# Head 0's path to the first expert gathers is reordered: output products, search over the corner of the sums, sample mixing, softmax halves

## The reference, cut to what matters

```python
h = rmsnorm(x)
gate_a, gate_b, z, xBC, dt, c_q, c_kv, k_rope = split(h @ w_in)
A = ssd_branch(z, xBC, dt)          # gated, group-normed, @ w_ssm_proj
B = mla_attention(c_q, c_kv, k_rope, cached pages)   # @ w_mla_proj
x = x + (sigmoid(gate_a) * A + sigmoid(gate_b) * B) @ w_out
x = x + peer(rmsnorm(x))
# peer, for each of 8 heads:
q = tb @ wq;  s1, s2 = q[:128] @ keys0, q[128:] @ keys1
sc1, i1 = top_k(s1, 16);  sc2, i2 = top_k(s2, 16)
sc, sel = top_k(sc1[:, None] + sc2[None, :], 16)     # 16 of 256 sums
idx = i1 * 128 + i2 at sel                            # 16 of 16384 experts
out += sum_k softmax(sc)_k * gelu(u[idx_k] . tb) * v[idx_k]
```

## Time and profile before

| | us |
|---|---|
| median of 3 runs | 2122.85 |
| lowest and highest | 2122.74, 2126.36 |
| span of the profiled execution, first to last instruction | 2118.6 |

### The profile page before, as it was taken

The page is one execution under the profiler, slowest core; times in us unless marked ns, Lnnn a source line. Parts: engine busy times, 40 slices in busy tenths (PEclk is TensorE's granted clock), DMA queues, the critical chain, the costliest instruction groups (busy, mean ns, idle before and its releaser), DMA issues. The chain is left out here.

```text
span 2118.6 us, 30049 instructions
## 1 busy us (share of the span) xinstructions
PE 1662.1 (78%) x10874; PEld 845.5 (40%) x10874; DVE 1452.1 (69%) x3622; ACT 487.8 (23%) x1411; POOL 670.6 (32%) x614
## 2 busy tenths in 40 slices
PE   7999999878787666666789998997777876676665
PEld 6888667523332111111168876773332421111111
DVE  3557543878778878878736565447877878887786
ACT  2246211211111221111222542112121112111112
POOL 0011000444454444444300110004454444444442
PEclk9999999977887676766799999999787876667668
DMA  5458896999999999999844688969999999999997
GB/s 203 149 203 301 288 382 258 365 411 420 419 413 420 403 419 421 420 417 417 361 177 159 215 319 280 387 240 407 404 420 412 421 419 399 421 421 420 412 417 307
DMA packets 135936, 749.04 MB, mean 354 GB/s; under 512 B 16611, under 2 KB 17100, under 8 KB 57298
## 3 DMA queue, kind: packets, MB, share of 16 engines
q0 software_dynamic: 84640, 588.54, 68.0%
q1 hardware_dynamic: 51138, 158.48, 20.7%
HBM read 735.63 MB, written 11.52 MB: 353 GB/s over the span
## 5 line engine op out<-in xcount | busy, mean ns | idle before, releaser
L1218 PE MATMUL ps<-arena 64*64 64x512 f32 x4096 | 743.4, 826 | 388.5 <-DVE arena L1832 386.6
L2454 POOL DMA_INDIRECT arena<-in_peer_uv,arena x528 | 622.9, 1180 | 784.1 <-PE ps L1218 636.6
L1823 DVE CUSTOM_DVE_ANT_0 arena<-arena,h 128x1024 f32<-128x1024 f32 x512 | 627.3, 1225 | 247.8 <-DMA arena<-in_peer_uv,arena 242.0
L1218 PEld LDWEIGHTS ps<-arena 64*64 64x64 f32 x4096 | 139.8, 164 | 938.7 <-DVE arena L1832 891.5
L572 PE MATMUL ps<-ht_tok,wring 128*128 128x264 f32 (+1 forms) x1536 | 363.5, 395 | 2.7 <-DMA wring<-in_w_in 2.7
L2195 ACT ACTIVATE arena<-arena 128x1 f32<-128x1 f32 x528 | 105.8, 203 | 978.6 <-DVE arena L1823 977.4
L572 PEld LDWEIGHTS ps<-ht_tok,wring 128*128 128x128 f32 x1536 | 293.7, 194 | 72.7 <-issue 16.9
L1832 DVE TENSOR_SCALAR arena<-consts,arena 128x64 f32<-128x64 f32 (+1 forms) x528 | 164.7, 312 | 15.0 <-ACT arena L2195 14.8
L572 PE MATMUL ps<-arena,wring 128*128 128x264 f32 x256 | 63.9, 393 | 0.3 <-DVE arena L1533 0.3
L2431 POOL DMA_DIRECT2D nrow<-in_norm_ffn x2 | 1.1, 533 | 184.9 <-PE ps L922 184.9
L572 PE MATMUL ps<-arena,gate 128*128 128x256 f32 x256 | 58.9, 382 | 0.0
(11 more groups left out here) (373 smaller groups left out, 1796.7 us busy)
## 6 DMA issues: line engine op xcount, KB each, us to landing
arena<-in_pages SPq DMA_DIRECT2D x256, 272.0 KB, 5.0
wring<-in_w_in SPq DMA_DIRECT2D x36, 1024.0 KB, 4.9
arena<-in_peer_uv,arena POOLq DMA_INDIRECT x528, 12.8
h<-in_state_ssm POOLq DMA_DIRECT2D x16, 512.0 KB, 6.5
out<-h POOLq DMA_DIRECT2D x16, 512.0 KB, 6.4
wring<-in_w_ssm_proj SPq DMA_DIRECT2D x8, 1024.0 KB, 10.7
arena<-in_w_out SPq DMA_DIRECT2D x8, 1024.0 KB, 9.6
wring<-in_peer_wq SPq DMA_DIRECT2D x8, 1024.0 KB, 9.7
```

Of the source, the lines that this page charges most:

```text
L1218: last = pe.matmul(ps[to:to + 64, SUM_BANK[t] + i, :], diag[rows, n % DIAGS, 0:64], ring[rows, HOME[n % RING], cols], start=n in TILE_FIRS ...
L1823: dve.tensor_tensor_reduce(ring[:, HOME[k], 0:D_MODEL], ring[:, HOME[k], 0:D_MODEL], tokens, 1.0, 0.0, ALU.mult, ALU.add, dots[:, column(n ...
L2454: pool.indirect_dma_start(ring[:, HOME[k], :], None, table, bass.IndirectOffsetOnAxis(ap=idx[:, TOPK * u + j:TOPK * u + j + 1], axis=0)).t ...
```

## The change

In the loop over half caches:
- `y_sums` moves from i = 1 to i = 0, ahead of `half_turns`, `keys(3)` and `vv(0)` swap places in i = 1; `y_inverse` and `y_normed` are spread over i = 1 to 3, and `ssm_first(0)` and `ssm(0)` wait for their half of the chunks each. ACT gets an Exp of one column behind the Sqrt, so that its table is back early.
- `prompt_scores` becomes a fused add and maximum per head from PSUM; the reduce in `prompt_maxima` goes. `prompt_probs` is split into two fours of heads.
- ACT copies the newest sample latent to `lat_kept` in i = 4.

In the passage:
- `out(0, 0)` waits for `mixed` alone; the turn of sample statistics stands behind it; the samples' mixing moves behind `out(3, 0)`. ACT squares the first tile by quarters as they are added; DVE writes the normed rows in two halves, and `ph_ready` counts each.
- Head 0's queries (in two halves of chunks for the first) and scores come straight after the turns, ahead of `sample_heads`, `sample_mla_parts` and `sample_mla`, which now stand between the second tile's products.
- Head 1's queries stand behind `out_samples` and ahead of `out(3, 1)`, its scores behind it.
- The first eight experts come from the 8 x 8 corner of the sums; the second eight maxima, the 256 sums and the second eight experts follow (`first_experts`). `best_experts(1)` starts at n = 4. `sample_gated` moves to n = 0 of the experts' loop, behind `inputs(0)`; the other late pieces follow at n = 1 to 8.
- Head 0's query weights are loaded as soon as the newest scores are there, ahead of head 4's. Gather 6 waits for `out_samples(1)`, gather 7 for `out(3, 1)`.
- Turns of the normed rows read 128 contiguous columns (`peer_wq` is laid out on the host to match); a block of zeros is added to the constants and not used; rows are projected one step later (`STEPS`).

```diff
@@ PROMPT tables
-    0: [("keys", (1,))], 1: [("keys", (3,)), ("y_sums", ())], 2: [("vv", (1,)), ("scores", (0, 0))],
+    0: [("keys", (1,)), ("y_sums", ())], 1: [("vv", (0,))], 2: [("vv", (1,)), ("scores", (0, 0))],
-    0: [("keys", (2,))], 1: [("vv", (0,))], 2: [("scores", (0, 1))],
+    0: [("keys", (2,))], 1: [("keys", (3,))], 2: [("scores", (0, 1))],
-PROMPT_PROBS = {4: 0, 9: 1}
+PROMPT_PROBS = {4: [(0, 0)], 5: [(0, 1)], 8: [(1, 0)], 9: [(1, 1)]}
@@ PE, the passage
-pe.wait_ge(sem("half_sums"), 1)
-...
+pe.wait_ge(sem("mixed"), 1)
+out(0, 0)
+pe.wait_ge(sem("half_sums"), 1)
+b = aux.fill()
+turn(ps[0:SAMPLES, b, 0:P], fin[:, 128:136], P)
+aux.filled(turn(ps[0:SAMPLES, b, P:2 * P], fin[:, 136:144], P))
+out(1, 0)
+out(2, 0)
+pe.wait_ge(sem("sample_weights"), 1)
+b = aux.fill()
+aux.filled(turn(ps[:, b, 0:SAMPLES], fin[0:SAMPLES, 384:512], SAMPLES))
+out(3, 0)
+samples_mixed()
+first_rows(0)
+samples_turned()
+first_rows(1)
+queries(0, 0, 0, P)
+queries(0, 1, 0, P)
+scores(0, (0,))
+sample_heads()
+out(0, 1)
+sample_mla_parts()
+out(1, 1)
+sample_mla()
+out(2, 1)
+pe.wait_ge(sem("mixed"), 2)
+out_samples(0)
+out_samples(1)
+queries(1, 0, 0, P)
+queries(1, 1, 0, P)
+out(3, 1)
+scores(1, (0,))
+...
@@ DVE, the loop
+for k in range(2):
+    hh = q + 4 * k
+    last = dve.tensor_tensor_reduce(sc[:, hh, 0:width], ps[:, b, 2 * P * k:2 * P * k + width], mask, 1.0, -3e38, ALU.add, ALU.max,
+                                    amax[:, hh:hh + 1])
-then(dve.tensor_reduce(amax, sc[:, :, 0:P * (t + 1)], AX.X, ALU.max))
@@ DVE, the passage
+def first_experts():
+    dve.wait_ge(sem("scores_out"), SCORES_AT[0, 0])
+    halves = [keysc[:, 0, 0, half, :] for half in range(2)]
+    for k in range(2):
+...
+        width = 8 * (k + 1)
+        sums = cand[:, 0:width * width]
+...
+        expert_numbers(k, width)
@@ DVE, late_tiles(n)
+if n == 0:
+    sample_gated()
+elif n == 1:
     out(2, 1)
 elif n == 2:
+    for half in range(2):
+        copy4(hp[2][:, half * 512:(half + 1) * 512])
+elif n == 3:
+    out(3, 1)
+elif n == 4:
     for half in range(2):
...
@@ SP
+sp.wait_ge(sem("lat_stores"), 64)
+sp.wait_ge(sem("lat_kept"), 1)
+sp.wait_ge(sem("aux_full"), marks["newest_scored"])
+sp.dma_start(wq_latents, w_q[0]).then_inc(sem("latents_load"), 16)
 sp.dma_start(wq_home, w_q[4]).then_inc(sem("home_load"), 16)
-sp.wait_ge(sem("lat_stores"), 64)
-sp.wait_ge(sem("wide_full"), marks["samples_mixed"])
-sp.dma_start(wq_latents, w_q[0]).then_inc(sem("latents_load"), 16)
 sp.wait_ge(sem("wide_full"), marks["mla_parts"])
 sp.dma_start(wq_spare, w_q[1]).then_inc(sem("spare_load"), 16)
```

More of the change, by code:

```diff
@@ L79, in projection_steps @@
     for first in range(3):
-        steps[7 + first] = [("rows", first)]
+        steps[8 + first] = [("rows", first)]
     for hh in range(2, P_HEADS):
         begun = TOPK * (hh - 2) - (2 if hh == P_HEADS - 1 else 0)
-        at = (2, 6, 10) if hh > 2 else (11, 12, 14)
+        at = (2, 6, 10) if hh > 2 else (12, 13, 14)
         steps[begun + at[0]] = [("queries", hh, 0, 0, TOKENS)]
@@ L1689, in _ @@
                                            cst("eye")[0:SAMPLES, 0:SAMPLES * A_HEADS].rearrange("p (b h) -> p b h", b=SAMPLES), ALU.mult))
-                    def out(k, t):
-                        b = aux.read()
-                        xs = x[:, t, k * BLOCK:(k + 1) * BLOCK]
-                        aux.emptied(dve.tensor_tensor(xs, xs, ps[:, b, 0:BLOCK], ALU.add))
                     def px_mean(t, columns):
@@ L1721, in _, with px_mean, px_rows @@
                         aux.emptied(dve.tensor_copy(ht[:, 4 * q:4 * q + 4, 0:P], ps[:, b, :].rearrange("p (c t) -> p c t", c=4)))
-                    def first_eight(k):
+                    def px_mean(t, columns):
+                        dve.wait_ge(sem(f"px{t}_squares"), 1)
+                        dve.tensor_scalar(st[:, columns], st[:, columns], 1.0 / D_MODEL, EPS, ALU.mult, ALU.add).then_inc(sem(f"px{t}_squares_mean"), 1)
+                    def px_rows(tiles):
+                        dve.wait_ge(sem(f"px{tiles[0]}_root"), 1)
+                        then(dve.reciprocal(st[:, 51 + tiles[0]:52 + tiles[-1]], st[:, 48 + tiles[0]:49 + tiles[-1]]))
+                        for t in tiles:
+                            last = dve.scalar_tensor_tensor(out=hp[t], in0=x[:, t, :], scalar=st[:, 51 + t:52 + t], in1=nrow[:, :], op0=ALU.mult, op1=ALU.mult)
+                        last.then_inc(sem("ph_ready"), 1)
@@ L2098, in y_root @@
                         act.activation(yroot, ymean, ACT.Sqrt).then_inc(sem("y_root"), 1)
+                        act.activation(st[:, 60:61], ones[:, 0:1], ACT.Exp)
                     prompt_keys(0)
@@ L2137, in _, with partial_squares @@
                     act.activation(st[:, 60:61], ones[:, 0:1], ACT.Sqrt)
+                    def partial_squares(k):
+                        cols = slice(k * BLOCK, (k + 1) * BLOCK)
+                        return act.activation(hp[0][:, cols], x[:, 0, cols], ACT.Square, accum_out=st[:, 54 + k:55 + k])
+                    for k in range(3):
+                        act.wait_ge(sem("aux_free"), 4 + marks["out", k, 0])
+                        last = partial_squares(k)
+                    last.then_inc(sem("px0_squares"), 1)
+                    act.wait_ge(sem("aux_free"), 4 + marks["out", 3, 0])
+                    partial_squares(3).then_inc(sem("px0_squares"), 1)
+                    act.wait_ge(sem("px0_squares_mean"), 1)
+                    act.wait_ge(sem("px0_squares"), 2)
+                    act.activation(st[:, 48:49], st[:, 57:58], ACT.Sqrt, scale=1.0 / D_MODEL, bias=st[:, 45:46]).then_inc(sem("px0_root"), 1)
                     b = wide.read()
@@ L2199, in _ @@
                     scores_out(0, (0,))
+                    b = wide.read()
+                    wide.emptied(act.copy(ot[:, :, SEQ:TOKENS], ps[:, b, 0:4 * SAMPLES].rearrange("p (q b) -> p q b", q=4)))
+                    for half in range(2):
+                        b = wide.read()
+                        wide.emptied(act.copy(mla_parts[:, half * 512:(half + 1) * 512], ps[:, b, :]))
+                    exponents(0)
                     queries_out(1, 0, 0, P)
@@ L2202, in _ @@
                     scores_out(1, (0,))
-                    exponents(0)
                     def late_tiles(n):
```

235 lines of the change are left out of this document (128 added, 107 removed).

## The result

The changed kernel takes **2142.43 us** (median of 4 runs, 2139.65 to 2143.28) against 2123.14 of the kernel before on the same chip. The ratio is 1.0087, with a 95% interval of 1.0074 to 1.01: slower by 18.5 us (the two medians lie 19.3 apart; differences are taken from the ratios throughout). The forecast was 2117.7 with a range of 2111 to 2126.5, so sign and size were both wrong. The profiled execution has a span of 2138.1 and a time of 2139.65.

The account below looks back on a forecast made before the run. The prediction took the expert gathers as bound by DMA bytes, so only less DMA idle time before 400 us helps. Loop -5.9 and passage 2 x 0.4 made -5.1: 2122.85 to 2117.7 us, range 2111 to 2126.5.

Parts of the forecast that it names:

- The loop: Loop over half pages: DMA idle time before 245 us pulled forward, -5.9 us for both layers, between 0 and 7.7.
- (e): Loop: ssm(0) waits for the last two y_normed chunks, which stand behind half_turns(3) on DVE; loss 1.2 us.
- (c): Loop, head maxima: fused add-and-max replaces the reduces, 3.4 against 5.3 us for large ones; PE's 1.56 wait goes.
- (d): Loop: PE's 1.74 us wait for the multiplication by inverse sums, cut in two, second half still in the way; gain 0.9.
- (f): Loop: whether PE's clock still falls behind its shortened waits for DVE was left open; worth 0 to 3.4 us.
- added table switches: Loop, ACT: Exp preload behind the group norm's Sqrt, done by about 225.6 us, ahead of exponentials at 226.5; cost 0.
- PE's order in the passage: Passage, layer 0: reordered products, queries and shorter search issue the first gather at 364.15 instead of 373.20 us.
- Rival B: Starved ring: second mixed waits for gather 0, PE stands, gather 8 late; +10.9 us, 2133.8; chance 0.13.
- The queue is dry only at 398: nothing is lost: Experts stage: gather 8 issued at 392.8 to 394.8 us, before the gather queue runs dry; no loss.
- the ledger: Passage, DMA bytes from 345 to 400 us: 13.4 MB end at 398.8 to 402.0; +0.4 us per layer taken.
- C: Nothing net: page loads already limit the loop and the passage comes out even; 2120 to 2127; chance 0.3.

Follow-up runs that it names:

- e1_gelu_first: The changed kernel with gelu(0) and gelu(1) put ahead of ACT's copies of head 1's queries and scores; 1.0054 of the kernel before.
- k1_gathers_later: e3_steps_back with the first four gathers held until the samples' first output product and sample_gated ahead of slot 0 on DVE; 1.0047 of the kernel before.
- e3_steps_back: e1_gelu_first with sample-row copies and sums earlier on DVE, and later tiles' mean, rows, turns and head 2's queries at their old slots; 1.0022 of the kernel before.
- k4_passage_alone: The changed kernel with the old loop over half pages, so passage, search and experts-stage places alone; 1.0139 of the kernel before, median 2155.11 us.
- e4_loop_alone: The kernel before with the new loop over half pages and nothing else; 0.9967 of the kernel before, 7.0 us faster.
- k2_corner_alone: e4_loop_alone with head 0's search over the 8 x 8 corner, in the old passage order; 0.9962 of the kernel before.
- h3_blocks_earlier: e3_steps_back with the samples' heads and parts ahead of head 0's queries on PE and ACT, releasing four weight blocks earlier; 1.0017 of the kernel before.
- h2_loop_light_filler: e4_loop_alone with one idle, unread PE matmul behind the output products of slots 0 to 6; 0.9961 of the kernel before.

## Why the prediction was wrong, point by point

**The loop: right.** It was put at -5.9 us, and alone it measures -7.0 (interval -10.6 to -3.4). How it splits over the layers one trace can't tell: the forecast took 3.6 us in layer 0, and the executions with the new loop reach `mixed` there between 2.5 (`e1_gelu_first`) and 6.2 us (`k1_gathers_later`) sooner than the kernel before. Its parts, in the timeline of the kernel after:

```profile
240.96 2.05 PE L574 MATMUL ps<-arena,wring 128*128 128x264 f32 x8 [1.37 <-DVE arena L1558]
...
253.35 0.66 PE L583 MATMUL ps<-consts,arena 128*128 128x128 f32 x4 [1.04 <-DVE arena L1596]
...
296.67 1.07 PE L986 MATMUL ps<-arena 128*32 128x256 f32 x16 [0.21 <-DMA arena<-in_pages]
```

(e) was put at a loss of 1.2 and is the first line, 1.37. The wait of 1.56 for the maxima (c) is gone; the fused instruction on 256 columns takes 0.42, as priced. The second line is the multiplication by the inverse sums for the first tile, where 0.61 stood before; the wait of 1.74 for the second tile, which (d) had left half in the way, is gone. PE now waits for pages, which it did not before: the third line, one of two waits of 0.5 us together. The doubt in (f) resolved well, as the clock stays at 1.00. The added table switches cost nothing: ACT's preload ends at 224.6, and the next group of exponentials starts behind DVE at 225.4. The Trainium skill, "ScalarE: Activation LUTs", section "What ACT_TABLE_LOAD costs", adds a drain of about 1380 ns to each such load. It is seen neither ahead of the load at 381.18 above, which follows a copy that ends at 381.08, nor behind it, where the activation starts at 382.48. In layer 0 the newest positions' scores start 5.9 us earlier (329.79 against 335.74).

**PE's order in the passage: right up to head 1's scores.** The forecast's times have the old loop in them, so they are compared from `mixed` on (335.20 in the kernel before). First gather: forecast 29.0 (364.15), measured 29.3. End of head 1's scores on PE: forecast 51.4 (386.6), measured 51.4 (380.67). Rival B did not come: DVE reads gather 0 at 364.89, and `out_samples` starts at 369.32 without a wait. Gather 8 is where it fails: forecast 57.6 to 59.6 (392.8 to 394.8), measured 65.1. That it stands at 394.38, within the forecast's figures, is only because the loop ended 6 us sooner. The first gathers came slowly beside the blocks: by DVE's reading of them in `e3_steps_back`, which waits for each, gathers 1 to 4 are 5 to 6.5 us apart (370.19, 376.73, 381.71, 386.68). The two queues of the changed kernel between 370 and 380:

```profile
q0 software_dynamic: 289, 2.11, 50.5%
q1 hardware_dynamic: 289, 2.11, 50.1%
```

The Trainium skill, "DMA: Bandwidth & Descriptors", section "Queues, rings and completion order", says that an engine takes turns between its queues, packet by packet; the trace agrees, with 2.11 MB for each.

**The step that failed on ACT.** The prediction said: "`exponents(0)` moves ahead of head 1's copies on ACT and ends near 372; head 1's queries reach it at 380: 0." It looked at the exponents and not at what is queued **behind** the copies on the same engine, `gelu(0)`. In the kernel before that order is harmless: the copies are over at 375.5, and the first dots arrive at 385.6. In the new order the dots are there at 366 and the copies last until 381. The wait of 11.06 us, with what follows from it, is worth 7.0 us (`e1_gelu_first`); with the second wait under it and the later places 13.8.

**The step that failed under it.** "DVE adds them at n = 4, behind gather 4's landing (385 to 389) and three search steps of head 1 (1.9): 391.8 to 393.9". That is 50 to 54 us after `mixed` for the landing. In `e1_gelu_first`, where nothing else holds DVE, gather 4 is read 56.9 after it and gather 8 issued 64.2 after it, against 57.6 to 59.6. The landing was put 3 us or more too early beside the blocks, and its price was not counted: "nothing is lost".

**The step that failed in the sum.** "The queue is dry only at 398: nothing is lost" was wrong twice. The queue did run out where it was put, 63 us after `mixed`, but gather 8 was not there:

```profile
392.00:396.00 4.00, 3.94 (x24) 1.30 (x28) 3.33 (x14) 3.56 (x6) 1.32 (x2) 0.57 0.04 14
```

And the ledger ended at 400. It counted bytes up to there and took for granted that what follows runs as before. What then decides is whether slots 8 to 27 are used up as fast as gathers land. In them PE has, besides 20 output products, three groups of turns, head 2's and head 3's queries and scores, and DVE and ACT wait on each other in every slot. The kernel before just keeps pace: share 1.00. The changed kernel starts this chain later (first output product 62.8 us after `mixed` instead of 57.0, the later tiles' rows 76.5 instead of 64.7), runs much of it at half clock, and is 14 us of DMA time behind in each layer.

**The ledger's gain was not one.** +0.4 was put for the passage of each layer, between -1.2 and +2.0; the passage costs +14.8 by `k4_passage_alone` and +12.8 by the difference of the changed kernel and `e4_loop_alone`. Earlier gathers were treated as time won unless bytes took it back. `k1_gathers_later` and `k2_corner_alone` show that the start of the gathers is all but off the path that sets the end: 13.3 us later costs 2.7 per layer, 2.9 us earlier gives nothing that can be told.

**Rivals.** None of the three named this. B had the right place (slots 0 to 8) and the right consequence (PE stands, the clock falls, gather 8 late) but the wrong wait, and its price of 8.4 us per layer was too low by a third or more. Its own wait does show in `h3_blocks_earlier` (2.02 us). C was refuted in its first half: the loop's gain is real.

What stays open: why the low clock lasts 20 us in the new passage and 7 in the old. The rows show that in `e3_steps_back` PE is busy 19.8 of 25 us from 395 to 420 and in `e4_loop_alone` 20.4 of 25, at granted clocks of 0.59 and 0.86. That is not the same amount of work, since a product takes 1.98 us at half clock: 86 matmuls against 108. Which of clock and waits came first in that stretch the rows do not tell. Also open is whether sharing with the blocks costs anything by itself. Nor is it settled what each of the later places costs alone; and no version of the new passage was found that beats the old one. The fastest kernels are the old passage with the new loop, `e4_loop_alone` (0.9967), `k2_corner_alone` (0.9962) and `h2_loop_light_filler` (0.9961), which can't be told apart.

## What to carry to other kernels

When a step is moved forward on one engine, list for every other engine what is programmed behind the instructions that serve it; an order that is free while data come late becomes a wait once they come early. Compare rows of two traces from a common row just ahead of the change, not from the start of the span; gather 8 looked right by its time from the start and was 6 us late. Do not end the budget of a ring at the moment it is full: find the row in which the consumer catches up (here DVE reading head 2's scores) and ask whether that row moves, since a producer that starts earlier is worth nothing if it doesn't. And take waits away one at a time on the chip, because the largest one (11 us on DVE) had a second of 8 (on PE) under it.

## What the runs showed of the hardware

I had not expected that idle work on PE can pay, nor that its length decides. Seven slots with 1.98 us of unread matmuls took 8.7 us off `e3_steps_back` (clock 0.75 to 0.91 from 395 to 465) and added 10.8 us to `e4_loop_alone`, where 0.98 us per slot changed nothing that can be measured. Gathers that started beside four 1 MB weight blocks landed some 5 us apart instead of 2.5 (DVE's waits for them in `e3_steps_back`: 3.07, 2.83 and 3.52 us for gathers 1 to 3), with 2.11 MB for each queue in 10 us; taking the sharing away gained nothing that can be told (`h3_blocks_earlier`). And executions of one loop ended up to 3.7 us apart, while the distance from `mixed` to the first gather was 29.25 or 29.26 us in each layer of the eleven traces that have that passage unchanged up to there.
